# Second layer of a two-layer decoder trunk: two query-weight chunks of the first token half projected one window later, so that four chunks are loaded once for both halves

## What is computed

```python
def short_conv(h, w_in, conv_w, w_out):          # layer 1
    bcx = h @ w_in                                # 1024 x 3072: six chunks of 512 columns
    b_gate, c_gate, xin = bcx[..., :D], bcx[..., D:2 * D], bcx[..., 2 * D:]
    return (b_gate * conv3(c_gate * xin)) @ w_out # 1024 x 1024: two chunks

def peer_ffn(h, w_q, sub_keys, u_tab, v_tab):    # after the mixer of either layer
    q = (xt @ w_q).reshape(T, 8, 2, 128)          # 1024 x 2048: four chunks, two heads each
    s = einsum('thpd,hpkd->thpk', q, sub_keys)    # 128 keys a half
    ...                                           # top 16 of each half, top 16 of the 256 sums: idx, gates
    act = gelu(einsum('chkd,cd->chk', u_tab[ib], xb)) * gb
    return einsum('chk,chkd->cd', act, v_tab[ib])
```

## Time and profile before

| what | value |
|---|---|
| median of 3 runs | 1563.86 us (1562.68 to 1564.55) |
| profiled execution | 1566.35 us, of it 1564.5 us span |
| granted TensorE clock, mean | 0.98 |
| moved by DMA | 630.26 MB, mean 403 GB/s |
| of it gathered expert rows | 536.90 MB in 512 DMAs |
| of it weights through SyncE's queue | 85.21 MB |

### The profile page before, as it was taken

How to read it: one execution, slowest core, us unless ns; L and a number is a source line. 1 busy time by engine, 2 the same in 40 slices (tenths; PEclk the granted TensorE clock), 3 DMA queues, 4 the chain that set the end, 5 groups by cost and what they waited for, 6 DMA issues and landing times.

```text
span 1564.5 us, 13166 instructions
## 1 busy us (share of the span) xinstructions
PE 1351.2 (86%) x3288; PEld 573.4 (37%) x3288; DVE 1004.9 (64%) x2452; ACT 595.2 (38%) x1809; POOL 572.4 (37%) x516
## 2 busy tenths in 40 slices
PE   8899899898987989897888998989878798877777
PEld 3454344443433434332333343434333243322222
DVE  5677878586576955454477975454566867764544
ACT  1334354534342524333334443333334344343333
POOL 0034334353333324333334343434443444444341
PEclk9999999999998999999999999999999999999999
DMA  9569999999999999999999999999999999999996
GB/s 395 242 244 418 418 400 371 418 420 419 419 420 419 363 416 420 418 422 420 420 420 418 408 415 419 420 420 420 421 420 420 418 408 421 421 421 421 421 422 278
DMA packets 94826, 630.26 MB, mean 403 GB/s; under 512 B 10528, under 2 KB 10656, under 8 KB 27424
## 3 DMA queue, kind: packets, MB, share of 16 engines
q0 software_dynamic: 73728, 536.90, 83.1%
q1 hardware_dynamic: 19296, 85.21, 13.6%
q10 hardware_dynamic: 1728, 7.31, 1.2%
HBM read 628.33 MB, written 1.05 MB: 402 GB/s over the span
## 4 chain that ended last, share of the span: by engine, by line
DMA 43%; PE 34%; DVE 13%; ACT 5%; issue 4%; POOL 1%; SPq 0%; ACTq 0%; DVEq 0%; POOLq 0%
DMA ring<-in_peer_uv_dram,idx 42%; PE acc L594 22%; PE pp L355 9%; DVE ring L1347 6%; ACT diag L909 1%; ACT weight L905 1%; PE acc L355 1%; DMA ring<-in_w_qkv_dram 1%; PE tt L370 1%; PE ss L429 1%; ACT gelu L903 1%; POOL ring L689 1%; ACT rows L731 1%; ACT L903 0%; DVE top_i L1076 0%
## 5 line engine op out<-in xcount | busy, mean ns | idle before, releaser
L594 PE MATMUL acc<-ring,diag 128*128 128x512 f32 x2048 | 996.2, 612 | 159.8 <-ACT diag L909 147.4
L1347 DVE CUSTOM_DVE_ANT_0 ring<-ring,xf 128x1024 f32<-128x1024 f32 x512 | 626.9, 1226 | 485.7 <-DMA ring<-in_peer_uv_dram,idx 476.0
L689 POOL DMA_INDIRECT ring<-in_peer_uv_dram,idx x512 | 572.2, 1118 | 971.5 <-PE acc L594 852.2
L594 PEld LDWEIGHTS acc<-ring,diag 128*128 128x128 f32 x2048 | 373.3, 193 | 709.4 <-issue 694.6
L903 ACT ACTIVATE gelu<-dots 128x1 f32<-128x1 f32 x512 | 103.6, 202 | 832.8 <-DVE dots L1347 832.2
L909 ACT ACTIVATE diag<-const,weight 128x128 f32<-128x128 f32 x512 | 205.4, 401 | 16.7
L905 ACT ACTIVATE weight<-gelu,gates 128x1 f32<-128x1 f32 x512 | 150.8, 295 | 16.6
L355 PE MATMUL pp<-stream,xT 128*128 128x512 f32 x192 | 96.8, 593 | 0.0
L355 PE MATMUL pp<-stream,rows 128*128 128x512 f32 x160 | 82.6, 598 | 0.0
L355 PEld LDWEIGHTS pp<-stream,xT 128*128 128x128 f32 x192 | 36.5, 191 | 45.6 <-issue 45.6
L355 PEld LDWEIGHTS pp<-stream,rows 128*128 128x128 f32 x160 | 30.6, 193 | 37.6 <-issue 37.6
(11 more groups left out here) (137 smaller groups left out, 716.7 us busy)
## 6 DMA issues: line engine op xcount, KB each, us to landing
stream<-in_peer_w_q_dram SPq DMA_DIRECT2D x44, 512.0 KB
stream<-in_conv_w_in_dram SPq DMA_DIRECT2D x40, 512.0 KB
stream<-in_w_qkv_dram SPq DMA_DIRECT2D x16, 512.0 KB
ring<-in_peer_uv_dram,idx POOLq DMA_INDIRECT x512
ring<-in_w_qkv_dram SPq DMA_DIRECT2D x3, 2048.0 KB, 24.4
stream<-in_w_o_dram SPq DMA_DIRECT2D x8, 512.0 KB
stream<-in_conv_w_out_dram SPq DMA_DIRECT2D x8, 512.0 KB
kept<-in_w_qkv_dram SPq DMA_DIRECT2D x1, 2048.0 KB
```

What stands on the lines that cost most here:

```text
L594: mm = nc.tensor.matmul(acc[half][:, :], diag[:, s % RING, :], row[:, D + half * 512:D + (half + 1) * 512], start=(k == 0), stop=(k == SLO ...
L689: nc.gpsimd.indirect_dma_start(dst, None, uv_dram, bass.IndirectOffsetOnAxis(idx[:, at:at + 1], 0)).then_inc(landed, 16)
L1347: nc.vector.tensor_tensor_reduce(row[:, 0:D], row[:, 0:D], xf[:, s // SLOTS % 2, :], 1.0, 0.0, ALU.mult, ALU.add, dots[:, s % RING:s % RIN ...
```

## The change

Two chunks more are shared in layer 1, input chunk 2 and query chunk 2. The first half's query chunks 2 and 3 leave window 2 (slots 240 and 254) and are projected in window 3's stretch, at slots 280 and 304, between the second half's input chunks. Place 6 holds (2, "in", 2), used by windows 2 and 3, and then (2, "wq", 2), used by both. Place 7 holds input chunk 5 and then (2, "wq", 3) in the same way. The input chunks of window 3 now come in the order 2, 4, 5, 3, 0, 1. The output projection is split into halves of four slots, the first of which needs only the first half of its input. In window 1 the keys' input chunk 3 changes places with the values' chunk 5 and starts at slot 43, the second half of the attention begins at 58 instead of 48, and the attention's value product uses the PSUM banks of the scores (`ss`) instead of those of the projections (`pp`). The core of the diff:

```diff
-    dict(q0=12, k0=22, q1=30, k1=46,
+    dict(q0=12, k0=22, q1=30, k1=56,
          logits0=24, bias0=25, max0=29, exp0=30, diff0=34, turn0=37, values0=40,
-         logits1=48, bias1=49, max1=53, exp1=54, diff1=58, turn1=61, values1=64,
-         norm0=45, norm1=66, gain=52, y0=49, y1=70, out0=73, out1=81, h0=82, f0=83, h1=90, f1=91, scale=91,
+         logits1=58, bias1=59, max1=63, exp1=64, diff1=68, turn1=71, values1=74,
+         norm0=45, norm1=76, gain=54, y0=49, y1=80, out00=68, out10=72, out01=82, out11=86, h0=86, f0=87, h1=90, f1=91, scale=91,
          wq0=94, wq1=104, wq2=116, wq3=128),
     dict(x=3, in2=8, in4=16, in3=24, in5=32, in0=40, in1=48, z0=26, z1=42, turn_z0=27, turn_z1=43, turn_g0=49, turn_g1=57,
-         conv0=30, conv1=46, times=59, out0=62, out1=70, h0=71, f0=72, h1=79, f1=80, scale=80,
-         wq0=84, wq1=98, wq2=112, wq3=126),
+         conv0=30, conv1=46, gain=20, times0=55, times1=59, out00=62, out10=66, out01=70, out11=74, h0=74, f0=75, h1=78, f1=79,
+         scale=79, wq0=84, wq1=98, wq2=152, wq3=176),
+    dict(x=3, in2=8, in4=16, in5=32, in3=40, in0=56, in1=64, z0=26, z1=50, turn_z0=27, turn_z1=51, turn_g0=65, turn_g1=73,
+         conv0=30, conv1=54, gain=20, times0=67, times1=75, out00=68, out10=73, out01=77, out11=81, h0=81, f0=82, h1=85, f1=86,
+         scale=86, wq0=90, wq1=106, wq2=132, wq3=156),
 )
-AT[2]["gain"] = 20
-AT = AT + (dict(AT[2], wq1=106, wq2=132, wq3=156),)
...
-RANK_PIECES = {(0, 1): 2, (0, 2): 2, (0, 3): 1, (1, 0): 2}
-LATE_IN_PROJECT = {2: 9, 1: 17, 3: 33, 5: 41}
+RANK_PIECES = {(0, 1): 2, (0, 2): 2, (0, 3): 1, (1, 0): 2, (3, 0): 2}
+LATE_IN_PROJECT = {2: 9, 1: 17, 5: 33, 3: 43}
 SHARED = {(1, "in", 0), (1, "in", 4), (1, "in", 5), (1, "out", 0), (1, "wq", 3),
-          (3, "in", 5), (3, "out", 0), (3, "wq", 3)}
+          (3, "in", 2), (3, "in", 5), (3, "out", 0), (3, "wq", 2), (3, "wq", 3)}
...
-        loads += [(2, "in", 2, STREAM), (2, "out", 0, 8), (2, "in", 4, STREAM), (2, "in", 5, 7), (2, "in", 3, STREAM), (2, "in", 0, STREAM),
-                  (2, "in", 1, STREAM), (2, "out", 1, STREAM), (2, "wq", 0, STREAM), (2, "wq", 3, 6), (2, "wq", 1, STREAM),
-                  (2, "wq", 2, STREAM)]
-        loads += [(3, "in", 2, STREAM), (3, "in", 4, STREAM), (3, "in", 3, STREAM), (3, "in", 0, STREAM), (3, "in", 1, STREAM),
-                  (3, "out", 1, STREAM), (3, "wq", 0, STREAM), (3, "wq", 1, STREAM), (3, "wq", 2, STREAM)]
+        loads += [(2, "in", 2, 6), (2, "out", 0, 8), (2, "in", 4, STREAM), (2, "in", 5, 7), (2, "in", 3, STREAM), (2, "in", 0, STREAM),
+                  (2, "in", 1, STREAM), (2, "out", 1, STREAM), (2, "wq", 0, STREAM), (2, "wq", 1, STREAM)]
+        loads += [(3, "in", 4, STREAM), (2, "wq", 2, 6), (3, "in", 3, STREAM), (2, "wq", 3, 7), (3, "in", 0, STREAM), (3, "in", 1, STREAM),
+                  (3, "out", 1, STREAM), (3, "wq", 0, STREAM), (3, "wq", 1, STREAM)]
...
-            return pp if n else ff
+            return ss if n else ff
...
-                for c in range(2):
-                    yield at[f"out{c}"]
-                    if c == 0 and n == 1:
-                        copied(pe, tt, (1, "y", 0), (1, "y", 1))
-                    elif c == 0:
-                        pe.wait_ge(yT_ready, n - 1)
-                    yield from project(pp, n, "out", c, yT, at[f"out{c}"])
+                for half in range(2):
+                    for c in range(2):
+                        yield at[f"out{c}{half}"]
+                        if c == 0 and n == 1:
+                            copied(pe, tt, (1, "y", half))
+                        elif c == 0:
+                            pe.wait_ge(yT_ready, 2 * (n - 2) + half + 1)
+                        yield from project(pp, n, "out", c, yT, at[f"out{c}{half}"], range(HALF * half, HALF * (half + 1)))
```

More of the change, by code:

```diff
@@ L78 @@
 LATE_RANK_PROJECT = {1: 0, 2: 25, 3: 57}
-RANK_PIECES = {(0, 1): 2, (0, 2): 2, (0, 3): 1, (1, 0): 2}
-LATE_IN_PROJECT = {2: 9, 1: 17, 3: 33, 5: 41}
+HALF = KT // 2
+RANK_PIECES = {(0, 1): 2, (0, 2): 2, (0, 3): 1, (1, 0): 2, (3, 0): 2}
+LATE_IN_PROJECT = {2: 9, 1: 17, 5: 33, 3: 43}
 SHARED = {(1, "in", 0), (1, "in", 4), (1, "in", 5), (1, "out", 0), (1, "wq", 3),
-          (3, "in", 5), (3, "out", 0), (3, "wq", 3)}
+          (3, "in", 2), (3, "in", 5), (3, "out", 0), (3, "wq", 2), (3, "wq", 3)}
 QUARTERS = 4
@@ L288, in slot, with in_order @@
             return ring[:, ring_at(s), :], uv_in[ring_at(s)], 16 * (s // RING + 1)
+        def in_order(n):
+            return sorted(range(6), key=lambda c: AT[n][f"in{c}"])
         def values_pool(n):
-            return pp if n else ff
+            return ss if n else ff
         def query_rows(n, c):
@@ L359, in project_part, with project @@
                         mm.then_inc(quarter_used, 1)
-            def project(pool, n, what, c, src, at):
-                for k in range(KT):
-                    yield at + k
+            def project(pool, n, what, c, src, at, ks=range(KT)):
+                for i, k in enumerate(ks):
+                    yield at + i
                     project_part(pool, n, what, c, src, (k,))
@@ L565, in gated_input @@
                     turn_h(n, "x", c)
-                for i, c in enumerate((2, 4, 3, 5, 0, 1)):
+                for i, c in enumerate(in_order(n)):
                     yield at[f"in{c}"]
@@ L601, in _ @@
             sides = begun(late(1), late_input(2), turn_late("q", 0), late_input(1), turn_late("k", 0), attention(0), late(2),
-                          turn_late("q", 1), late_input(3), late_input(5), turn_late("k", 1), late(3), turn_mixed(0), attention(1), turn_mixed(1),
+                          turn_late("q", 1), late_input(5), late_input(3), turn_late("k", 1), late(3), turn_mixed(0), attention(1), turn_mixed(1),
                           output(1), turn_output(1), *(experts(1, c) for c in range(4)))
@@ L652, in _ @@
                         written(sp, pp, last_reader(*previous[place]))
-                    if place == 6:
+                    elif place == 6:
                         sp.wait_ge(logit_max, 4)
-                        written(sp, pp, (1, "values", 1))
+                        written(sp, values_pool(1), (1, "values", 1))
                     sp.dma_start(places[place], matrix_of(n, what, c)).then_inc(w_in[place], 16)
@@ L860, in new_gain @@
                 if n == 1:
+                    written(act, pp, (1, "in", 5))
                     written(act, pp, (1, "in", 3))
-                    written(act, pp, (1, "in", 5))
                 else:
@@ L883, in gated_input @@
                     copy_scaled((n, "x", c), xTm[:, 4 * c:4 * c + 4, :], gain_mix[:, first:first + 4])
-                for c in (2, 4, 3, 5, 0, 1):
+                for c in in_order(n):
                     yield at[f"in{c}"] + 8
@@ L912, in _ @@
             sides = begun(second_head(), late(1), late_input(2), turn_late("q", 0), late_input(1), turn_late("k", 0), attention(0),
-                          late(2), turn_late("q", 1), late_input(3), late_input(5), turn_late("k", 1), new_gain(1), late(3), turn_mixed(0),
+                          late(2), turn_late("q", 1), late_input(5), late_input(3), turn_late("k", 1), new_gain(1), late(3), turn_mixed(0),
                           attention(1), turn_mixed(1), output(1), *(experts(1, c) for c in range(4)), new_keys())
@@ L1321, in convolve @@
                     kk = slice(4 * c, 4 * c + 4)
-                    yield at["times"] + c
+                    yield at[f"times{c}"]
                     copied(dve, tt, (n, "g", c))
                     link(nc.vector.tensor_tensor(yT[:, kk, :], a[:, kk, :], qTa[:, kk, :], ALU.mult))
-                dve.sem_inc(yT_ready, 1)
+                    dve.sem_inc(yT_ready, 1)
             def finish(n):
```

## The result

The changed kernel took **1554.17 us** (median of 4 runs, 1553.87 to 1554.92) against 1563.27 us for the kernel before (4 runs, 1562.30 to 1564.55). That is 9.1 us less, inside the stated range, outside the forecast's own 1548.5 to 1552.5, and close to rival (a), bytes alone (1553.9). The ratio on record is 0.9923, 95% interval 0.9908 to 0.9938; the two medians give 0.9942, just outside that interval, and why they differ is not known. One later execution, of the kernel with output chunk 1 held back, took 1703.96 us in a slow run and is left out of the comparison.

The account below looks back on a forecast made before the run. DMA bound at about 420 GB/s, engines only where the rate dips. Terms -10.0 + 1.5 - 0.9 - 3.6 = -13.0 us on the profiled 1566.35 gave 1553.3, 1551 as a median; range 1544 to 1557.5.

Parts of the forecast that it names:

- rival (a): Whole kernel: bytes alone count, window 1 only trades its dip at slot 41 for one at 57 to 75; 1553.9 us, chance 0.27.
- The bytes: Layer 1, windows 2 and 3: two streamed chunks fewer, 4.19 MB at 420 GB/s, 10.0 us less DMA time.
- Kept loads in time: Slots 280 and 304: the 2 MB loads into kept places arrive before use, cost 0; far end 13 us at each place.
- Rival (d): Slots 264 to 335: TensorE sets the pace, late kept loads at 280 or 304; slower, 1568 us or so, chance 0.04.
- Window 3's stretch: Slots 264 to 335: the 16 projections moved here make TensorE lag where no loads pass; +1.5 us, bounds 0 and +6.
- The ring: Eight places of requested gathers, some 20 us of DMA work; 5 to 8 us can be given up before DMA idles.
- (c): Windows 3 and 1: TensorE gives much back, the no-load slots are not covered; 1556 to 1560 us, chance 0.12.
- Boundary 256: Window boundary at slot 256: a ranking and a projection leave it; -0.9 us, bounds -1.4 and +1.
- Boundary 128: Window boundary at slot 128: VectorE, then TensorE set the pace, none of that work moves; 0, bounds -3 and +3.
- Window 1: Slots 41 to 75: VectorE's old lag shrinks, a new TensorE lag comes; 6.6 idle us become 3.0, so -3.6 us.
- Boundary 384: Window boundary at slot 384: the same engine work as before, so 0.
- The median: Whole kernel: the median stands 2.5 us below the profiled execution, so 1551 us from a profiled 1553.3.

Follow-up runs that it names:

- the control: The changed kernel run once more without any edit, beside the single edits: 1555.28 us (8 runs), ratio 0.9948.
- the old table: The changed kernel with window 1's slot table as before the change, output projection still in halves, layer 1 as changed: 1554.10 us, ratio 0.9928.

## Why the prediction came out as it did

**The bytes: right.** 4.19 MB at 420 GB/s, 10.0 us, is what the change gives, adding as many bytes back took 8.7 to 10.6 us, and with layer 1's change alone the kernel stood 10.4 us under the one before. The rate hardly depends on the size of the DMAs here (422 and 419 GB/s).

**Kept loads in time: right.** The load for slot 280 was issued at 900.8 us, landed in 11.5 and was first read at 926.9; the one for slot 304 was issued at 972.3, landed in 11.5 and was first read at 998.3. No wait of TensorE for either is in the trace. Rival (d) had nothing for it.

**Window 3's stretch: +1.5 taken, 0 measured** (420 GB/s over 192 us). The ring covered slots without loads altogether, so (c) falls there. The sum had counted 80 projections in slots 264 to 335, where the table puts 75; with them TensorE needs 2.70 us a slot and not 2.76. Boundary 256: -0.9 taken; 391 GB/s (1.4 us) before, 413 (0.3 us) at 870 to 890 us after, so -1.1. Boundary 128: 0 taken, 5.6 to 4.5 measured (3.7 in the control), so -1.1.

**Window 1: -3.6 taken, -0.7 measured.** This is the step that failed. The old dip shrank from 6.6 to 0.9 us, as the count of VectorE's work had it. But the step priced the new lag in slots 57 to 75 by TensorE alone, 6 us, "of which the ring takes most". Its own sum gives more: 19 slots of 2.50 us are 47.5 us, not the 50 that it sets against 56, so the lag was some 9 us before the ring. And it left out ScalarE's exponentials, which the table moves from slot 54 to 64: 7.6 us without a diagonal, which ran under two loads before and under none after, and behind them TensorE at half its clock. The new dip is 5.0 us (3.5 in the control, with 2.3 left of the old one). The load moved back over it fills it; the old table trades it back. How the 5.0 divide between the block and TensorE's own lag stays open.

**Boundary 384: 0 taken, +1.7 measured** (2.8 at 1180 to 1215, less the 1.1 of the earlier trace rows at 1250 to 1290). "The same engine work" overlooked the entry (3, 0): 2 in `RANK_PIECES`, which is in the diff.

Put together: -10.0 + 0 - 1.1 - 1.1 - 0.7 + 1.7 = -11.2 by the windows, -13.0 forecast. The misses partly cancel: +2.9 in window 1 and +1.7 at boundary 384 against -1.5 in window 3's stretch, -1.1 at boundary 128 and -0.2 at boundary 256. That the sum came within 2 us is in part luck.

The median is off by more, 1554.2 against 1551. The profiled execution came out at 1554.41 where 1553.3 was forecast, 1.1 us over. The other 2.3 us come of taking 2.5 us off for the median: the changed kernel's profiled execution stood only 0.2 over its median. That 2.5 (3.1 with the fourth run) belonged to one execution of the kernel before, and what was slow in it isn't known.

Of the cases, the one at 0.27, (a), had it right, in the time and in its reason: window 1 traded one dip for the other. Its argument against itself, that the new lag starts with a full ring, did not hold, since the block lets it run dry.

## What to carry to other kernels

In a kernel bound by DMA, a load that is no longer made is worth its bytes over the rate, in pieces of 512 KB as of 2 MB; look for what can be shared first. Where an engine holds the gathers up for longer than the ring lasts, ask which transfers pass at that time: a step moved out from under a load starts to cost, and a load that isn't urgent, held back by one wait, can be the cover. Count every engine's work at the new place of a moved step, ScalarE's table loads too, and expect filled dips to come back in part at the next tight place. Compare two executions window by window before a difference of their spans is put down to an edit.

## What the runs showed of the hardware that was not expected

A filled dip is not time gained one for one: held back over window 1's block, output chunk 1 filled 3.5 us there, and the boundary of slot 128 lost 2.4 us more (356 GB/s); one piece of ranking a slot filled 1180 to 1215, and 1215 to 1270 lost 2.1.

The other thing is how much one and the same stretch varies. At 312 to 350 us, seven profiles of kernels that are alike up to there moved 358, 361, 363, 365, 365, 377 and 381 GB/s: 3.5 to 5.6 us of idle time. The first slot began at 102.2 to 102.4 us in nine of the fourteen profiles and at 103.2 to 104.0 in the other five. A single span of one of these kernels is therefore good to some 2 us, which is as much as most of the single edits gave.
